# A hybrid attention and convolution layer: five pieces of attention work change places between the projections

## What is computed

```python
proj = jnp.einsum('btd,de->bte', x, w_in)
q, k, v, g_att, gb, gc, hh, g_conv = jnp.split(proj, ...)
o_att = _dilated_attention(q, k_all, v_all, offset)      # branches (128,1), (512,4), (2048,16)
att = o_att * jax.nn.silu(g_att)
u = gc * hh
y_conv = conv_w[0] * u_pad[:, 0:t] + conv_w[1] * u_pad[:, 1:1+t] + conv_w[2] * u_pad[:, 2:2+t]
z = gb * y_conv * jax.nn.silu(g_conv)
out = jnp.einsum('bte,ed->btd', jnp.concatenate([att, z], -1), w_out)
y = _layer_norm(alpha * x + out, ln_g, ln_b)
```

## Time and profile before

| | us |
|---|---|
| median of 3 runs | 352.95 |
| lowest and highest run | 352.83, 353.74 |
| the profiled execution's own time | 351.81 |
| its span | 349.8 |
| TensorE busy in the span | 340.7 |
| VectorE busy | 210.1 |
| ScalarE busy | 123.8 |
| mean granted TensorE clock | 0.997 |

### The profile page before, as it was taken

One profiled execution on the slowest core, in us unless ns is written; L12 is line 12 of the kernel. 1 busy time (PEld: TensorE's weight loads), 2 busy tenths in 40 slices (PEclk: granted clock), 3 DMA queues, 4 the chain that ended last, 5 costly groups with the idle time before them and its releaser, 6 DMA issues.

```text
span 349.8 us, 7201 instructions
## 1 busy us (share of the span) xinstructions
PE 340.7 (97%) x2984; PEld 298.1 (85%) x2984; DVE 210.1 (60%) x406; ACT 123.8 (35%) x257; POOL 16.4 (5%) x40
## 2 busy tenths in 40 slices
PE   8999999999999999999999999999999999999991
PEld 6998988997989889979898899798879887888791
DVE  3745528955254657652546586525546699894884
ACT  5624424342244423423443334234453744400100
POOL 0130000000200000002000000020000001100000
PEclk9999999999999999999999999999999999999998
DMA  7999999999999999999999999999999999999995
GB/s 294 393 417 416 419 421 419 421 423 418 420 406 422 423 418 420 381 418 418 414 419 423 420 413 383 421 399 399 427 421 418 416 419 350 388 386 395 403 359 227
DMA packets 31714, 140.52 MB, mean 402 GB/s; under 512 B 3137, under 2 KB 3905, under 8 KB 26689
## 3 DMA queue, kind: packets, MB, share of 16 engines
q1 hardware_dynamic: 16034, 75.83, 53.3%
q10 hardware_dynamic: 15648, 64.23, 46.5%
HBM read 132.15 MB, written 71.86 MB: 583 GB/s over the span
## 4 chain that ended last, share of the span: by engine, by line
PE 94%; DVE 3%; ACT 1%; issue 0%; DVEq 0%; ACTq 0%
PE pj_b L1334 11%; PE pj_b L1336 10%; PE pj_b L1335 10%; PE pj_a L1334 9%; PE pj_a L1335 8%; PE pj_a L1336 8%; PE sc L1497 5%; PE sc L1530 4%; PE px L1682 3%; PE px L1684 3%; PE px L1683 3%; PE po L1477 3%; PE px L1445 3%; PE pt L1463 3%; DVE rg L1038 1%; PE sc L1362 1%
## 5 line engine op out<-in xcount | busy, mean ns | idle before, releaser
L1334 PE MATMUL pj_b<-x_hi,w_hi 128*128 128x320 f32 x248 | 78.5, 316 | 0.3 <-DVE mix L1054 0.3
L1335 PE MATMUL pj_b<-x_lo,w_hi 128*128 128x320 f32 x248 | 76.5, 308 | 0.0
L1336 PE MATMUL pj_b<-x_hi,w_lo 128*128 128x320 f32 x248 | 76.5, 308 | 0.0
L1334 PE MATMUL pj_a<-x_hi,w_hi 128*128 128x256 f32 (+1 forms) x248 | 71.3, 288 | 0.0
L1335 PE MATMUL pj_a<-x_lo,w_hi 128*128 128x256 f32 (+1 forms) x248 | 69.5, 280 | 0.0
L1336 PE MATMUL pj_a<-x_hi,w_lo 128*128 128x256 f32 (+1 forms) x248 | 69.5, 280 | 0.0
L909 DVE TENSOR_TENSOR w_lo<-w_raw,w_hi 128x1024 fp32r<-128x1024 f32 x30 | 37.1, 1235 | 26.8 <-ACT w_hi L573 26.8
L1334 PEld LDWEIGHTS pj_a<-x_hi,w_hi 128*128 128x128 f32 x248 | 46.8, 189 | 5.5 <-issue 3.7
L1334 PEld LDWEIGHTS pj_b<-x_hi,w_hi 128*128 128x128 f32 x248 | 46.5, 188 | 4.9 <-issue 3.6
L1336 PEld LDWEIGHTS pj_a<-x_hi,w_lo 128*128 128x128 f32 x248 | 46.7, 188 | 0.0
L1335 PEld LDWEIGHTS pj_a<-x_lo,w_hi 128*128 128x128 f32 x248 | 46.6, 188 | 0.0
(11 more groups left out here) (189 smaller groups left out, 477.1 us busy)
## 6 DMA issues: line engine op xcount, KB each, us to landing
k_buf<-in_k_used SPq DMA_DIRECT2D x16, 1280.0 KB, 12.3
v_buf<-in_v_used SPq DMA_DIRECT2D x20, 1024.0 KB, 14.5
out_k_used_out<-in_k_used ACTq DMA_DIRECT2D x16, 1280.0 KB, 17.7
out_v_used_out<-in_v_used ACTq DMA_DIRECT2D x17, 1024.0 KB, 16.2
w_raw<-in_w_tiles SPq DMA_DIRECT2D x30, 512.0 KB, 8.9
out_k_rest_out<-in_k_rest ACTq DMA_DIRECT2D x12, 1024.0 KB, 13.8
out_v_rest_out<-in_v_rest ACTq DMA_DIRECT2D x12, 1024.0 KB, 13.9
wo_raw<-in_w_out SPq DMA_DIRECT2D x8, 512.0 KB, 17.8
```

Of the source, the lines that this page charges most:

```text
L1334: nc.tensor.matmul(out, w_hi[:, w], x_hi[:, c], start=(k == 0), stop=False)
L1335: nc.tensor.matmul(out, w_hi[:, w], x_lo[:, c], start=False, stop=False)
L1336: return nc.tensor.matmul(out, w_lo[:, w], x_hi[:, c], start=False, stop=(k == KT - 1))
```

## The change

On TensorE, in rounds 0 to 2:

- `prompt_turn(i, 2)` moves from behind the first half of G_CONV to ahead of it, next to `sample_scores(i, 2)`.
- `prompt_values(i, 2)` and `sample_scores(i, 3)` move from behind the second half of G_CONV to between its halves, so that this second half and V stand next to each other.
- The second half of A moves up next to the first half; `sample_turn(i, 0)` and `(i, 1)` come behind both, and `turn_v(i + 1)` comes behind them, ahead of `sample_turn(i, 2)`.

In the last round `sample_values` stand in groups of four, four and two between the last projections instead of two, two, two and four. ScalarE and VectorE do the same work in an order that follows. No instruction is added or taken away.

```diff
--- before.py
+++ after.py
@@ -793,8 +793,8 @@
                 copy_next()
                 if i == 1:
                     copy_next()
+                move_prompt(i, 2)
                 exp_gate(t0 + G_CONV, 0)
-                move_prompt(i, 2)
                 copy_next()
                 exp_gate(t0 + G_CONV, 1)
                 split_hi(t0 + 5)
@@ -807,13 +807,13 @@
                 copy_next()
                 out_prompt(i)
                 exp_gate(gate_tile(i), 0)
-                rows_v(i + 1)
-                copy_next()
+                copy_next()
+                exp_gate(gate_tile(i), 1)
                 move_sample(i, 0)
                 move_sample(i, 1)
-                exp_gate(gate_tile(i), 1)
+                rows_v(i + 1)
+                move_sample(i, 2)
                 split_hi(t0 + 7)
-                move_sample(i, 2)
                 copy_q(i + 1)
                 copy_next()
                 split_hi(t0 + 8)
@@ -1158,16 +1158,16 @@
                 split_lo(t0 + 4)
                 z_read(i)
                 gate_half(i, 0, 0)
-                gate_half(i, 0, 1)
                 mask_sample(i, 3)
                 max_sample(i)
+                gate_half(i, 0, 1)
                 split_lo(t0 + 5)
                 norm_sample(i)
                 stage_v(i + 1)
                 split_lo(t0 + 6)
                 gate_half(i, 1, 0)
+                gate_half(i, 1, 1)
                 new_v(i + 1)
-                gate_half(i, 1, 1)
                 split_lo(t0 + 7)
                 copy_q(i + 1)
                 split_lo(t0 + 8)
@@ -1567,19 +1567,19 @@
                 project(t0 + B, 1)
                 prompt_values(i, 1)
                 sample_scores(i, 2)
+                prompt_turn(i, 2)
                 project(t0 + G_CONV, 0)
-                prompt_turn(i, 2)
+                prompt_values(i, 2)
+                sample_scores(i, 3)
                 pe.wait_ge(z_done, i + 1)
                 project(t0 + G_CONV, 1)
-                prompt_values(i, 2)
-                sample_scores(i, 3)
                 project(v_tile(i + 1), 0)
                 project(v_tile(i + 1), 1)
                 project(gate_tile(i), 0)
-                turn_v(i + 1)
+                project(gate_tile(i), 1)
                 sample_turn(i, 0)
                 sample_turn(i, 1)
-                project(gate_tile(i), 1)
+                turn_v(i + 1)
                 sample_turn(i, 2)
                 for t in range(V_PIECES):
                     sample_values(i, t)
@@ -1615,17 +1615,15 @@
                 sample_turn(i, 1)
                 project(t0 + G_CONV, 0)
                 sample_turn(i, 2)
-                sample_values(i, 0)
-                sample_values(i, 1)
+                for t in range(0, 4):
+                    sample_values(i, t)
                 pe.wait_ge(z_done, i + 1)
                 project(t0 + G_CONV, 1)
-                sample_values(i, 2)
-                sample_values(i, 3)
                 project(gate_tile(i), 0)
-                sample_values(i, 4)
-                sample_values(i, 5)
+                for t in range(4, 8):
+                    sample_values(i, t)
                 project(gate_tile(i), 1)
-                for t in range(6, V_PIECES):
+                for t in range(8, V_PIECES):
                     sample_values(i, t)
 
             for i in range(NPAIR - 1):
```

## The result

| | before | changed |
|---|---|---|
| median, us | 353.00 | 362.51 |
| lowest and highest of 4 runs, us | 352.83, 353.74 | 361.27, 363.06 |
| profiled execution, its span, us | 351.81, 349.8 | 363.06, 360.9 |
| mean granted TensorE clock of the profiled execution | 0.997 | 0.987 |

The ratio is 1.0274, with a 95% interval of 1.0241 to 1.0307. Slower was forecast, at 359.9 us; the time lies 0.7 us above the range.

A forecast was written before the change was run, and what follows sets the result against it. The prediction took TensorE to bound the kernel. Round 0 at +4.4 us, two rounds at +1.5 and the last at -0.5 summed to +6.9 on 352.95, so 359.9 us, with a range of 356.4 to 361.8.

The forecast's parts named there:

- What bounds: TensorE, busy 340.7 of 349.8 us: a microsecond it gains or waits is nearly everywhere one of the result.
- Boundaries: Fewer switches between pieces around G_CONV and A win some 0.3 us per round, 0.2 in the last, 1.1 in all.
- The gate of G_CONV: In rounds 0 to 2, V's second half waits 1.57 us for VectorE's product of the gate with the bank.
- Round 0: The third prompt turn waits 3.08 us for VectorE's late normalisation; with the other terms this round costs +4.4 us.
- The cover rule: Wait at V's second half is gate chain and hand-over, 4.40 us, less the first half of V as cover, 2.83.
- The sample turns: Behind A, the last sample turn keeps 0.1 us slack on its move: costed at nothing, up to 0.3 a round if gone.
- the last round: The 0.34 us idle before A's second half goes, with two boundaries at about 0.1: -0.5 us.
- The clock: Rival: TensorE's clock falls to half behind round 0's 3.1 us wait, giving 362.8 us; chance 0.04.
- The price of a fall: Behind round 0's wait, a half of G_CONV (2.94 us) takes twice as long at half clock: +2.9 us.

The follow-up runs named there:

- e9: The kernel before without the last two of 57 copies of used keys to output, part of the new key cache unwritten: 351.23 us beside 354.45, ratio 0.9913.
- e5: Changed kernel with e4's earlier weight load and third values and last scores behind both halves of G_CONV: 352.28 us beside 352.52 of before, ratio 0.9983.
- e1: Changed kernel with everything around G_CONV put back, leaving the parts around A and in the last round: 352.65 us beside 353.43 of before, ratio 0.9979.
- e6: e4 with the last sample scores back behind G_CONV's second half and the gate ahead of their mask on VectorE: 353.96 us beside 352.52, ratio 1.0037.
- e4: Changed kernel with round 0's fourth load of keys issued behind a weight load, so that weight tile lands earlier: 356.11 us, ratio to before 1.0072.
- e2: The kernel before with only the third prompt turn moved ahead of G_CONV's first half, and its move ahead on ScalarE: 356.24 us, ratio 1.0067.
- e8: The changed kernel itself run again, nothing altered, beside other experiments: 362.48 us, ratio to before 1.0267.
- e7: e4 with a second, unread reciprocal in G_CONV's second gate in rounds 0 to 2, lengthening V's wait: 368.12 us, ratio to before 1.0436.
- e3: Changed kernel with matmuls nobody reads put into its four waits (round 0's third turn, V's second half): 359.63 us, ratio to before 1.0164.
- e10: e5 without the same last two copies of used keys that e9 leaves out: 350.60 us, ratio to before 0.9894.

## Why the prediction was off

- *What bounds.* Right: a microsecond of TensorE is one of the result when it is lost. For a microsecond won it was incomplete: the copies hold the end behind TensorE's, by 3 us of the median (e9), and ate most of e5's gain. I had read the busy shares and not the last landings.
- *Boundaries.* A little too large: 0.17 us a round with both joints (e5), 0.03 with A's alone (e1), for the forecast 0.3 and 0.1, and some 0.3 in the last round for 0.2; 0.8 us in all for 1.1. In the changed order itself all groups but the waiting ones took 0.05 more a round, for 0.07 less.
- *The gate of G_CONV.* Right in place and releaser. From start to start, as the forecast counts, 1.60 us for 1.57 in rounds 0 and 2; 1.97 in round 1, with 0.36 of idle time of VectorE that is unexplained. The cover rule held when cover was given back (e6) and when the chain was lengthened (e7).
- *Round 0.* Right: 3.02 us for 3.08, released by line 1015, and gone when the one weight tile is loaded earlier (e4).
- *The sample turns, the last round.* Right: no wait, and -0.6 for -0.5.
- *The clock.* This is the step that failed. I rated it a rival of 0.04, and only behind round 0's wait. It fell behind that wait in every profile in which the wait stood (not in every run of e2, by the mean clocks), and once behind a wait of 1.8 us. Two falls at 1.6 and 1.5 us are 3.1 of the 4.4 us by which the profiled execution lies over the forecast for it (363.06 against 358.7); 0.4 is the start and 0.4 the longer chain of round 1. With the waits filled the ratio to before is 1.0164, where the forecast was 1.0197 and the changed kernel has 1.0267 to 1.0274. The reasoning behind it was a row in which TensorE was idle from 342.35 and the clock still at 1.00 at 346 to 347. I took that one case as saying that nothing happens behind a shorter one. It was one case of a delay that differs: 5.0 us after the idle stretch began there, 1.9 us in e2, 2.9 in round 0 of the changed kernel, 4.5 in e8. In e8 and in round 1 of the changed kernel it came after TensorE was back at work. Hence the rule of the Trainium skill, page "TensorE: Matmul & The Clock Gate", section "Why this matters for your kernels", which warns of idle gaps between bursts, was right against my row, and the trace agrees with it for the wait of 3 us.
- *The price of a fall.* I put it at +2.9, a whole half of G_CONV doubled; it was 1.5 to 1.6 where the clock stayed low for 3.4 us, since half of that time is lost and not the group's own length. So it is luck that the rival's 362.8 us lies 0.3 us from the median: its one fall at 2.9 stood for two at 1.5 to 1.6.

## What to carry to other kernels

Before joining two pieces of work, ask what the piece that moves away was covering: the wait is the length of the hand-over chain less what is left between, and here a moved piece of 2 us cost 1.6 to 2.0 us three times while the joint won 0.1 or less. Read also the round that differs, for a piece that just met its input has no slack to be moved earlier. Put an idle stretch of TensorE of 3 us down with about 1.6 us of low clock behind it (more in e2 and once in e7, where the clock stayed low for twice as long), and when TensorE's end moves earlier look at what lands last before counting the gain.

## What the runs showed of the hardware that was not expected

- The granted clock can fall after TensorE has resumed its work (146 to 147, idle until 145.96; in e8 at 60.0, idle until 58.62), and it stayed at 1.2 GHz for 3.4 us, or twice that (e2, once in e7), though TensorE was fully busy.
- Matmuls whose results nobody reads, put into a wait, kept the clock at 2.4 GHz: 3.6 us faster with 6.9 us more of work (e3).
- The mean clock of a run is no measure of such falls by itself: e5 has 0.989 in the profile with no low stretch before TensorE's last matmul, since the time behind TensorE's end counts as well.
- Two of 57 copies from memory to memory, 1.9% of the traffic, were worth 3 us of the median of before and most of its scatter (e9: 0.6 us for 2.75; e10, without the same copies, scatters over 2.1).
